# S5 state-space layer of a streaming-encoder trunk: smaller Toeplitz transfers, tiled strip products, and a rearranged scan of the states

## The reference, cut to what matters

```python
# 64 groups of 16 channels, 64 complex states each; f32 throughout
lam_bar = exp(lam * step)                       # (64, 64)
b_bar = ((lam_bar - 1) / lam)[..., None] * b
bu = einsum('blgn,gpn->blgp', u, b_bar)         # input into the states, 512 steps
states = scan(x[t] = lam_bar * x[t-1] + bu[t])
y = einsum('gnp,blgp->blgn', c, states).real + d * u
y = gelu(y)
y = y * sigmoid(y @ glu_w + glu_b)              # the "GLU" product
```

## Time and profile before

| | |
|---|---|
| median of three executions | 1279.61 us (1279.23 to 1279.71) |
| the profiled execution | 1278.21 us |
| its span | 1276.4 us |
| PE busy | 1240.6 us, 97% of the span |
| DVE busy | 671.7 us, 53% |
| ACT busy | 462.0 us, 36% |
| POOL busy | 64.8 us, 5% |
| granted TensorE clock, mean | 0.997 of full |

### The profile page before, as it was taken

One profiled execution on the slowest core, in us unless ns is written; L12 is line 12 of the kernel. 1 busy time (PEld: TensorE's weight loads), 2 busy tenths in 40 slices (PEclk: granted clock), 3 DMA queues, 4 the chain that ended last, 5 costly groups with the idle time before them and its releaser, 6 DMA issues.

```text
span 1276.4 us, 16013 instructions
## 1 busy us (share of the span) xinstructions
PE 1240.6 (97%) x6277; PEld 1034.5 (81%) x6277; DVE 671.7 (53%) x785; ACT 462.0 (36%) x486; POOL 64.8 (5%) x82
## 2 busy tenths in 40 slices
PE   3889999999999999999999999999999999999998
PEld 3778888888888888888888888888888888888886
DVE  8997754344444444646655465634454444444443
ACT  5635433333333333333333333422333333332232
POOL 6940000000000000000000000000000000000000
PEclk9999999999999999999999999999999999999999
DMA  5373333332312334323232133233232323323331
GB/s 115 100 144 123 99 99 99 99 99 90 105 58 90 105 90 138 107 66 107 66 99 83 57 107 96 69 96 93 74 119 80 102 94 99 99 68 90 93 110 66
DMA packets 141039, 121.03 MB, mean 95 GB/s; under 512 B 5720, under 2 KB 132880, under 8 KB 141008
## 3 DMA queue, kind: packets, MB, share of 16 engines
q1 hardware_dynamic: 138832, 116.40, 29.5%
q10 hardware_dynamic: 2176, 4.20, 1.7%
HBM read 114.29 MB, written 2.10 MB: 91 GB/s over the span
## 4 chain that ended last, share of the span: by engine, by line
PE 94%; ACTq 2%; ACT 2%; DMA 1%; DVE 1%; issue 0%; SPq 0%; DVEq 0%
PE bank L709 27%; PE bank L711 27%; PE bank L710 27%; PE bank L809 2%; PE bank L808 2%; PE bank L807 2%; ACTq L434 2%; DMA s<-in_x_dram 1%; PE bank L835 1%; PE bank L837 1%; PE bank L836 1%; PE bank L846 1%; PE bank L820 0%; PE bank L821 0%; ACT s_states L900 0%; PE bank L537 0%
## 5 line engine op out<-in xcount | busy, mean ns | idle before, releaser
L709 PE MATMUL bank<-u_hi,w_hi 128*128 128x512 f32 x960 | 374.9, 391 | 0.0
L711 PE MATMUL bank<-u_hi,w_lo 128*128 128x512 f32 x960 | 373.6, 389 | 0.0
L710 PE MATMUL bank<-u_lo,w_hi 128*128 128x512 f32 x960 | 373.5, 389 | 0.0
L1186 DVE TENSOR_TENSOR w_lo<-w_raw,w_hi 128x2048 fp32r<-128x2048 f32 x112 | 256.4, 2290 | 165.7 <-ACT w_hi L900 165.6
L900 ACT ACTIVATE w_hi<-w_raw 128x2048 fp32r<-128x2048 f32 x112 | 214.0, 1910 | 319.1 <-PE bank L711 314.0
L709 PEld LDWEIGHTS bank<-u_hi,w_hi 128*128 128x128 f32 x960 | 180.2, 188 | 37.8 <-issue 0.7
L710 PEld LDWEIGHTS bank<-u_lo,w_hi 128*128 128x128 f32 x960 | 180.2, 188 | 37.6 <-issue 0.5
L711 PEld LDWEIGHTS bank<-u_hi,w_lo 128*128 128x128 f32 x960 | 180.2, 188 | 37.5
L709 PE MATMUL bank<-h_hi,w_hi 128*128 128x512 f32 x352 | 136.9, 389 | 0.0
L710 PE MATMUL bank<-h_lo,w_hi 128*128 128x512 f32 x352 | 136.9, 389 | 0.0
L711 PE MATMUL bank<-h_hi,w_lo 128*128 128x512 f32 x352 | 136.9, 389 | 0.0
(11 more groups left out here) (220 smaller groups left out, 1321.6 us busy)
## 6 DMA issues: line engine op xcount, KB each, us to landing
w_raw<-in_ret_w_qkvg_dram SPq DMA_DIRECT2D x24, 1024.0 KB, 4.9
w_raw<-in_ffn_w_gate_dram SPq DMA_DIRECT2D x22, 1024.0 KB, 5.2
w_raw<-in_ffn_w_up_dram SPq DMA_DIRECT2D x22, 1024.0 KB, 5.1
w_raw<-in_ffn_w_down_dram SPq DMA_DIRECT2D x32, 704.0 KB, 4.1
w_raw<-in_ret_w_o_dram SPq DMA_DIRECT2D x8, 1024.0 KB, 5.1
w_raw<-in_s_glu_w_dram SPq DMA_DIRECT2D x4, 1024.0 KB, 5.5
s<-in_x_dram ACTq DMA_DIRECT2D x8, 256.0 KB, 8.5
s_w<-in_x_dram SPq DMA_DIRECT2D x1, 2048.0 KB, 7.6
```

Source lines behind the costliest of these rows:

```text
L709: pe.matmul(o, w_hi[w][:, w_cols], hi, start=first, stop=False)
L710: pe.matmul(o, w_hi[w][:, w_cols], lo, start=False, stop=False)
L711: return pe.matmul(o, w_lo[w][:, w_cols], hi, start=False, stop=end)
L1186: dve.tensor_tensor(w_lo[s][:, :], w_raw[:, s, :], w_hi[s][:, :].bitcast(F32), ALU.subtract).then_inc(w_lo_ready[s], 1)
```

## The change

In the S5 layer:

- **Toeplitz.** A DMA now carries both halves of a part (two windows of 16 partitions) and only the part of a window that isn't zero: 128, 112, 96, ... 16 KB for `r` = 0 to 7. It is 8 DMAs a part in place of 16. SP issues parts 0 and 1 alone; of parts 2 and 3 SP issues the even `r`, ACT the odd ones. The zeros are written by seven DMAs from a block of zeros, ahead of the load of `x_tok` in SP's queue, once the last `u` transposes are done.
- **Strips.** The two halves of a pair are made as two products of 64 rows by 16 columns, at rows and columns 0 and 64 of the array, in place of one of 128 rows by 32 columns with a half-empty `fb`. `fb` is then the input tables themselves, and ACT's four copies into it fall away. `strip_out` is two copies in place of one.
- **States copy.** `s5_input_out` writes with the pair `j` innermost, 4 elements side by side, where it wrote elements 256 bytes apart.
- **Scan.** The carries are kept in a tile of their own (`carries`). ACT copies the first carry into it (after `seg_done` 1) and the finished carries back into `states` (`ends`, after `seg_done` 2); DVE waits for the first, `y_states` for the second. The lift takes three real products in place of four: 4 instructions a quarter in place of 8. POOL makes the sum and difference of the powers for it, two more instructions ahead of its third block.
- **Weights.** The first unit of the GLU is loaded right behind part 0, and ACT and DVE split it earlier.
- **Order on PE.** Strips 5 now come after `y_inputs` 0 and 1, strips 6 after `y_inputs` 2 and 3, and strips 7 after `y_inputs` 4 and 5, which wait for part 2 of the Toeplitz transfers; both `y_states` come behind strips 7.

The diff, cut to its core:

```diff
-        def toeplitz_half(queue, part, half):
+        def toeplitz(queue, part, steps):
...
-            row = 2 * N * (part // 2) + N * half
-            for r in range(STEPS):
-                first = STEPS - 1 - r
-                queue.dma_start(toep[N * r:N * r + N, half, part, :, :, :].rearrange("p t j n -> p (t j n)"),
-                                strip[row:row + N, part % 2, first:first + STEPS, :, :].rearrange("p t j n -> p (t j n)")
+            rows16 = slice(2 * N * part, 2 * N * part + N)
+            for r in steps:
+                queue.dma_start(toep[N * r:N * r + N, :, part, r:, :, :].rearrange("p h t j n -> p h (t j n)"),
+                                strip[rows16, :, 0:STEPS - r, :, :].rearrange("p h t j n -> p h (t j n)")
                                 ).then_inc(toep_loaded[part], 16)
...
+            sp.wait_ge(zeros_set, 1)
+            b, fill = S5_AT[("u", 7)]
+            sp.wait_ge(bank_full[b], fill + 1)
+            for r in range(1, STEPS):
+                cols = r * PART * N
+                sp.dma_start(toep[N * r:N * r + N, :, :, 0:r, :, :].rearrange("p h q t j n -> p (h q) (t j n)"),
+                             repeated(zeros[:, 0:cols], 1, 2 * NPART)).then_inc(toep_zeroed, 16)
...
-            sp.wait_ge(pads_zeroed, 1)
+            toeplitz(sp, 0, range(STEPS))
+            sp.wait_ge(toep_zeroed, 16 * (STEPS - 1))
+            load_unit(0, 0, glu_v[:, :, 0:256], KT, 256)
+            toeplitz(sp, 1, range(STEPS))
+            toeplitz(sp, 2, range(0, STEPS, 2))
+            toeplitz(sp, 3, range(0, STEPS, 2))
             for part in range(NPART):
-                toeplitz_half(sp, part, 0)
-            for s in range(2):
-                for part in (s, 2 + s):
-                    sp.wait_ge(toep_loaded[part], 16 * 2 * STEPS)
-                load_unit(s, 0, glu_v[:, :, 256 * s:256 * s + 256], KT, 256)
+                sp.wait_ge(toep_loaded[part], 16 * STEPS)
+            load_unit(1, 0, glu_v[:, :, 256:512], KT, 256)
...
-                o = ps[2 * N * (k // 4):2 * N * (k // 4) + 2 * N, :]
+                o = [ps[64 * half:64 * half + N, :] for half in range(2)]
                 for i in range(JB):
                     for ri in range(2):
-                        pe.matmul(o[:, P * i:P * i + P], fb[:, ri, JB * k + i, :],
-                                  r_tc[:, ri, JB * k + i, :, :], start=(i == 0 and ri == 0), stop=False)
+                        for half in range(2):
+                            rows64 = slice(64 * half, 64 * half + 64)
+                            pe.matmul(o[half][:, P * i:P * i + P], fb[rows64, ri, JB * k + i, :],
+                                      r_tc[rows64, ri, JB * k + i, :, :], start=(i == 0 and ri == 0), stop=False)
...
-            pe.wait_ge(toep_loaded[0], 16 * 2 * STEPS)
+            pe.wait_ge(toep_zeroed, 16 * (STEPS - 1))
+            pe.wait_ge(toep_loaded[0], 16 * STEPS)
             y_inputs(0)
             y_inputs(1)
-            strips(6)
+            strips(5)
             pe.wait_ge(seg_done, 1)
-            pe.wait_ge(toep_loaded[1], 16 * 2 * STEPS)
+            pe.wait_ge(toep_loaded[1], 16 * STEPS)
             y_inputs(2)
             y_inputs(3)
+            strips(6)
+            pe.wait_ge(toep_loaded[2], 16 * STEPS)
+            y_inputs(4)
+            pe.wait_ge(seg_done, 2)
+            y_inputs(5)
             strips(7)
-            pe.wait_ge(seg_done, 2)
             y_states(0, 0)
-            pe.wait_ge(toep_loaded[2], 16 * 2 * STEPS)
-            y_inputs(4)
-            y_inputs(5)
             y_states(1, 1)
...
-                copy(states[:, 1:CH + 1, :, JB * SLOT[k]:JB * SLOT[k] + JB].rearrange("p c r j -> p j r c"),
-                     ps[:, :].rearrange("p (j r c) -> p j r c", j=JB, r=2)).then_inc(free, 1)
+                copy(states[:, 1:CH + 1, :, JB * SLOT[k]:JB * SLOT[k] + JB],
+                     ps[:, :].rearrange("p (j r c) -> p c r j", j=JB, r=2)).then_inc(free, 1)
...
-                if c == 1:
-                    act.wait_ge(fb_zeroed, 1)
-                    for ri in range(2):
...
-                            copy(fb[rows64, ri, :, N * half:N * half + N], b_tab[ri][rows64]).then_inc(fb_ready, 1)
...
             strip_out(1)
-            act.wait_ge(pads_zeroed, 1)
-            toeplitz_half(act, 0, 1)
             strip_out(2)
             strip_out(3)
...
-            toeplitz_half(act, 1, 1)
             strip_out(4)
             strip_out(5)
-            toeplitz_half(act, 2, 1)
+            toeplitz(act, 2, range(1, STEPS, 2))
+            act.wait_ge(seg_done, 1)
+            copy(carries[:, :, 0], seg_ends[:, 0]).then_inc(carry0_ready, 1)
             strip_out(6)
             act.activation(small[:, 25:26], eps[:, :], ACT.Gelu_apprx_tanh)
+            split_weights(0, 0)
+            act.wait_ge(seg_done, 2)
+            for ri in range(2):
...
             strip_out(7)
-            toeplitz_half(act, 3, 1)
+            toeplitz(act, 3, range(1, STEPS, 2))
...
+                step(mul(lifted_diff, repeated(carry_diff[:, part], 2, M), repeated(seg_powers[:, 1, 0:M, js], 1, M)))
+                step(mul(lifted, repeated(carries[:, part], 2, M), repeated(lift_pair[:, :, :, js], 1, M)))
+                settle()
+                into = seg[:, 1:SEG, 0:M, :, js]
+                step(dve.tensor_tensor(into, into, repeated(lifted_diff, 3, 2), ALU.add))
+                settle()
+                dve.tensor_tensor(into, into, lifted, ALU.add).then_inc(scan_done, 1)
```

More of the change, by code:

```diff
@@ L641, in _ @@
             strips(4)
-            strips(5)
             def y_pairs(k):
@@ L959, in strip_out @@
                 ps, free = s5_full("strip", k)
-                rows32 = slice(2 * N * (k // 4), 2 * N * (k // 4) + 2 * N)
-                copy(strip[rows32, k % 4 // 2, STEPS - 1:, JB * (k % 2):JB * (k % 2) + JB, :],
-                     ps[rows32, :].rearrange("p (j t n) -> p t j n", j=JB, t=STEPS)).then_inc(free, 1)
+                js = slice(JB * (k % 2), JB * (k % 2) + JB)
+                for half in range(2):
+                    last = copy(strip[2 * N * (k // 2):2 * N * (k // 2) + N, half, :, js, :],
+                                ps[64 * half:64 * half + N, :].rearrange("p (j t n) -> p t j n", j=JB, t=STEPS))
+                last.then_inc(free, 1)
             act.wait_ge(rs_ready, 1)
@@ L1364, in _ @@
                 dve.wait_ge(bank_free[b], fill + 1)
-            seg = states[:, 1:CH + 1, :, :].rearrange("p (s i) r j -> p s i r j", s=SEG)
             w = step8[:, :, :, :].rearrange("p a r j -> p a (r j)")
@@ L1382, in _ @@
             dve.wait_ge(seg_done, 1)
[L1384 to L1385 removed]
             for n in range(1, SEG - 1):
[L1387 to L1389 removed]
+                if n == 1:
+                    for a in range(2):
+                        step(mul(carry_tmp[:, a], seg_ends[:, 0], step64[:, a]))
+                else:
+                    step(mul(carry_tmp, repeated(carries[:, :, n - 1], 1, 2), step64))
                 settle()
[L1391 to L1392 removed]
+                step(dve.tensor_tensor(carries[:, :, n], seg_ends[:, n], carry_tmp[:, 0], ALU.add))
                 settle()
[L1394 to L1395 removed]
+                last = dve.tensor_tensor(carries[:, :, n], carries[:, :, n], carry_tmp[:, 1][:, :, ::-1, :], ALU.add)
                 if n < SEG - 2:
@@ L1400, in _ @@
             dve.wait_ge(seg_done, 2)
+            dve.wait_ge(carry0_ready, 1)
+            step(dve.tensor_tensor(carry_diff, carries[:, :, :, 0, :], carries[:, :, :, 1, :], ALU.subtract))
+            settle()
             JH, M = J // 4, SEG - 1
@@ L1765, in segment_powers @@
                         settle()
-                last.then_inc(lift_ready, 1)
-                pool.wait_ge(lift_ready, 1)
+                step(last)
+                settle()
+                pool.wait_ge(tb_ready, 1)
+                lift = [seg_powers[:, i, 0:SEG - 1, :] for i in range(2)]
+                pool.tensor_tensor(lift_pair[:, :, 0, :], lift[0], lift[1], ALU.subtract).then_inc(lift_ready, 1)
+                pool.tensor_tensor(lift_pair[:, :, 1, :], lift[0], lift[1], ALU.add).then_inc(lift_ready, 1)
+                pool.wait_ge(lift_ready, 2)
             for n, k in enumerate(POOL_BLOCKS):
```

101 lines of the change are left out of this document (44 added, 57 removed).

## The result

| | before | after |
|---|---|---|
| median of 6 runs (lowest to highest) | 1279.66 us (1278.60 to 1280.90) | 1285.09 us (1283.63 to 1285.32) |
| ratio to before | | 1.0039 (1.0028 to 1.0049) |
| profiled run: its time, its span | 1278.21, 1276.4 us | 1285.31, 1283.5 us |
| first product of the GLU | 101.86 us | 108.96 us |

The change makes the kernel slower by 5.4 us. The forecast was 1278.6 with a range up to 1282.8, so the result lies outside it, on the side to which it gave 0.20. The two profiled spans differ by 7.1 us, and so do the starts of the GLU: as the prediction had it, nothing behind that point moved, and the search is for 7.1 us ahead of it. (The medians differ by less, since the profiled execution of the kernel before lies 1.5 us under its median and that of the change 0.2 over.)

The account below looks back on a forecast made before the run. Ahead of the GLU's first product (101.86 us), ACT's Toeplitz issues delay the first gelu; moving it from 89.50 to 88.5 gains 1.0: 1278.21 - 1.0 = 1277.2, or 1278.6 as a median (profiled run 1.4 under). Range 1275.6 to 1282.8.

Parts of the forecast that it names:

- the price of the transfers: Toeplitz parts 2 and 3: four issues take 3.1 us; part 2 lands 5.3 us behind its first issue, about 79.8.
- The walk: Timeline from strips 2 at 56.3 us to the first gelu at 88.5 against 89.50: 1.0 us gained.
- Rival (d): Transfers slower, both queues reading the same 16 partitions: part 2 lands 7 behind, +1.7, 1280.3; chance 0.12 with Rival (c).
- Rival (c): PE's clock at half speed after idling 2.4 us before `y_inputs` 4: +1.7, 1280.3; chance 0.12 with Rival (d).
- Rival (e): Nothing gained on the path: dearer landing and issue (+0.9) eat the gain, 1279.5; chance 0.50 together with the forecast.
- The reordering: On PE: strips 5 gain just 0.6 us behind `y_inputs`; PE waits 2.4 us for part 2, strips 7 standing behind.
- The strips: One strip on PE takes 2.38 us (2.21 to 2.56) against 2.21 before, the two halves running side by side.
- rival (b): Strips serialised on PE: 3.7 us in place of 1.86 for the first part, five on the path, 1287.9; chance 0.08.
- The states copies: ACT's copies of the states fall from 1.0 to 0.5 us each; the other end is the old 1.0.
- The scan: DVE's scan begins at about 52.9 us against 54.30 and ends its seven steps at 71.8.
- The lift: DVE's lift takes some 3.55 us a quarter against 4.2, ending at 92.5; its gain is off the path.
- The zero fill: Zeros ahead of `x_tok` in SP's queue: 18 us from 33 to 51 at 102 GB/s, x at 58.6, in time.

Follow-up runs that it names:

- experiment 4: The changed kernel with ACT's DMAs of parts 2 and 3 reading rows of parts 0 and 1, 64 partitions away: 1277.91 us, ratio 0.9987.
- experiment 1: The changed kernel with PE's order of before (strips 5 ahead of `y_inputs` 0 and 1, strips 7 ahead of 4 and 5): 1279.61 us, ratio 0.9997.
- experiment 3: The changed kernel without the seven zero-fill DMAs and the waits for them: 1283.76 us, ratio 1.0032.
- experiment 6: The changed kernel with PE's order of before, parts 2 and 3 issued by SP alone, and zeros by column: 1276.35 us, ratio 0.9972.
- experiment 7: The kernel before with only the new states copy, pair `j` innermost: 1278.69 us, ratio 0.9991.
- experiment 2: The changed kernel with all eight DMAs of parts 2 and 3 issued by SP, none by ACT: 1282.04 us, ratio 1.0019.
- experiment 5: The changed kernel with zeros written by column, over all partitions from 16n on, in seven DMAs of the same bytes: 1284.75 us, ratio 1.0036.
- experiment 8: The changed kernel with 14 extra products ahead of PE's wait for part 2 and 18 ahead of the first transposes: 1283.46 us, ratio 1.0028.

## Why the prediction was wrong, point by point

- **The step that failed** is the price of the transfers under "The walk": "Four issues took 2.73 us ... and 3.50 ... with both queues at work ...; I take 3.1", and "I take 3.0: landed at 74.5 + 5.3 = 79.8 or so". They measured 5.2 and 5.6, and 7.8. The rows it took them from are of two queues that together read 32 partitions and moved 160 to 168 GB/s. The change brings the bytes down to 0.56 and the source partitions to 16, at 91 to 102 GB/s, so it wins nothing in time, and the rows of before were no neighbours. Experiment 4, which only moves the source, gives 3.4 and 5.8 and brings the GLU to 101.02, with 100.9 predicted. This term costs 5.0 us directly. It costs this much only together with the new order on PE: the median is back at or under that of the kernel before when either of the two is taken away (experiments 1 and 4).
- **Rival (d)** had the mechanism, "both queues now read the same 16 partitions", and a landing of 7. It got a chance of 0.12 together with (c), and its price left out that the blocked queue holds ACT itself. **Rival (c)** came true as well, twice instead of once; the two are not independent, since the longer wait brings the lower clock. (c) and (d) should have been one case, with the 5.0 us and the 3.0 of the clock, so 8 us and not 1.7 each. That (d)'s 102 GB/s is the rate that was measured is luck: it was read from the pace at which one queue of the kernel before issued, when the two together moved 160 GB/s and more.
- **Sums that don't come out.** Rival (e) has "landing and issue at their dearer ends (+0.9)"; by the ends that the walk names, 7.0 for 5.3 and 3.5 for 3.1, it is +2.1. (c) and (d) together are 1278.6 + 1.7 + 1.7 = 1282.0, and with strips at 2.56 1282.9, not 1282.8 and 1282.5. Set right, neither reaches 1285.09.
- **The reordering** was seen to bite ("strips 7, which are free to go, stand behind them") and priced at 2.4 us of waiting for part 2; it was 3.59, and the order alone is worth 5.5 us of medians (experiment 1).
- **The strips** were dearer in the forecast than in the trace: 2.15 for 2.38. 32 instructions take 1.86 us, 0.06 each, so the halves do run side by side in one bank, and rival (b) is out. The rule of the Trainium skill (TensorEngine Tiling (Array Packing), Gotcha 1) that speaks against it isn't borne out: by it the 1.86 would be about double. The small diagonal overlaps fully (0.29 from start to start, for 16 instructions).
- **The states copies** came out at 0.60 for 0.5, with before at 1.0: the nearest row was a good one. For PE the gain does stay hidden behind POOL (strips 2 wait 1.67 and 1.77 us for it in experiments 3 and 6), though experiment 7 leaves room for 1 us, and in experiment 6 they lie on the chain, ahead of the scan.
- **The scan** began 3 us later than forecast, at 55.86 behind 2.36 us of waiting. The stall of PE in front of it was not foreseen; it costs little in the change, as strips 2 are just 0.9 late.
- **The lift** took 3.5 us a quarter as predicted (81.06 to 84.56), and DVE waits 0.76 for the first carry. Its gain is off the path in the change, as said; in experiment 6 its first quarter is on it.
- **The zero fill** took from 33.8 until about 53.25 us at 100 to 117 GB/s, and `x_tok` landed at 61.6, 8.9 us behind its issue and 3 us later than rival (d) had it. The weight load of the first transpose of x waited 0.2 us for it, so it costs next to nothing here, but it was in time by no margin.

## What to carry to other kernels

Before a DMA is costed by its bytes, count the partitions it reads and writes. Here about half the bytes on half the source partitions saved no time, and a second queue on the same partitions only added issues that held the engine that made them. Never put work that is ready behind a wait whose length is the least known term; and cost a wait on PE together with the clock that it brings down. When several fixes end at the same wait, try them together before one is called worthless: by the medians experiment 2 gave 3.0 us alone, 1 gave 5.5, 5 nothing measurable, and the three together 8.7. That is no more than the sum, so what the third adds is not shown by the medians; the trace of experiment 6 shows it on the chain.

## What the hardware showed beyond the forecast

- **SBUF to SBUF transfers on sixteen partitions went at about 100 GB/s**: with 16 as source 91 to 106 GB/s, with two queues (change) or one (experiment 2), and with source and destination of 16 each 100 to 117 in the zero fill; spread over up to 112 partitions the same bytes went at up to 280. The Trainium skill, SBUF — State Buffer, Door 1: The DMA port swizzle, has partitions 0 to 15 reach 4 ports, 104 GB/s measured; the rows agree, and the prediction had overlooked it. The Trainium skill, SBUF — State Buffer, "Can I just issue two DMAs to hit both halves?", says no, with 6% gained. Experiment 4 differs: with the two queues on sources 64 partitions apart, the stretch at 76 to 78 us moved 180 GB/s in place of 98, and issue to release fell from 7.8 to 5.8 us. The measurement decides, for transfers inside SBUF.
- **An issue can hold the engine that makes it.** ACT's eight issues of the change took 0.59 to 2.61 us, median 1.15; in experiment 4, with the same DMAs on other source partitions, 0.59 to 1.09, median 0.84.
- **Instructions come by DMA too, and can come late.** In the change a packet of 16 KB on the instruction queue ran at 48.1 to 49.0 us, into the stall of 2.11 us, which begins at 48.3. In the kernels without the stall (before, experiments 3, 5, 6 and 7) such a packet begins at 41.6 to 43.2 us and the next at 47.2 to 49.2; in those with it (the change and experiments 1, 2, 4 and 8) none begins from 40 to 47 us, and one does at 47.2 to 48.4, 0.1 to 0.4 us before PE stops. So one came some 5 us late while the fill kept the DMA engines busy. Runtime: NRT & Kernel Launch, Instruction fetch mechanics, in the Trainium skill tells of refills in blocks of 16 KiB by the sequencer's own DMA queue, mostly hidden; this one was not. The fill's part in it is shown; that PE stood for want of this packet is the reading that fits, and no run varied the fetch itself.
- **When the clock fell.** Full speed gave way to the lower level behind waits of 3.59 and 4.74 us (change), 4.54 and 4.42 (experiment 3), 5.14 and 4.73 (experiment 5) and 3.13 (before, and the earlier trace rows), and stayed in experiments 4 (1.54, 1.71) and 6 (none over 2). In between it goes either way: it stayed behind 3.35 us in experiment 2 and 2.61 in experiment 7, and fell behind 2.09 in experiment 5; the stall of 2.1 us at 49 was followed by a fall at 50.55 in the profile of experiment 2 and by none in those of the change and of experiments 1, 4 and 8; and in experiment 1 the clock fell behind a wait of 1.90 us, with 1.74 and 2.21 a little ahead of it. How it decides stays open.
